# Expert rows added to gathered residual rows in each block, instead of a combine stage at the end

## What is computed

```python
h = rms_norm(x, g_norm_ffn) * (1 + sc_m) + sh_m
g_prob, g_idx = top_k(softmax(h @ w_router_group), 1)       # 1 of 4 groups
e_prob, e_idx = top_k(softmax(logits of this group), 2)     # 2 of its 8 experts
weight = g_prob * e_prob / sum(e_prob)
y[token] += weight * (silu(h @ w_gate[e]) * (h @ w_up[e])) @ w_down[e]   # both experts
x = x + gt_m * y                                            # gate gt_m: one row for prompt, one for sample
```

## Time and profile before

| | us |
|---|---|
| median of 3 runs | 1254.57 (1252.77 to 1256.62) |
| profiled execution | 1249.39, of which the span of the trace is 1247.6 |
| TensorE busy | 1070.9 (86% of the span) |
| VectorE, ScalarE, GpSimd busy | 554.3, 252.5, 186.9 |
| mean granted clock of TensorE | 0.924 |

### The profile page before, as it was taken

One profiled execution on the slowest core, in us unless ns is written; L12 is line 12 of the kernel. 1 busy time (PEld: TensorE's weight loads), 2 busy tenths in 40 slices (PEclk: granted clock), 3 DMA queues, 4 the chain that ended last, 5 costly groups with the idle time before them and its releaser, 6 DMA issues. The chain is left out here.

```text
span 1247.6 us, 13856 instructions
## 1 busy us (share of the span) xinstructions
PE 1070.9 (86%) x4732; PEld 690.1 (55%) x4732; DVE 554.3 (44%) x1110; ACT 252.5 (20%) x595; POOL 186.9 (15%) x267
## 2 busy tenths in 40 slices
PE   4699999999298889989999994399999999999920
PEld 1245555544255455657666753377777777777610
DVE  2345556554363555566575736511222121222147
ACT  1132232222222222332223201011111111111100
POOL 1122222222501101110110000110110011011032
PEclk9799999999677999999999985599999999999975
DMA  8985555441331122221120105649999999999857
GB/s 316 335 304 195 190 189 188 171 154 44 116 88 59 33 78 76 77 93 35 59 74 4 51 34 222 250 155 363 361 375 368 359 371 374 360 363 369 303 193 262
DMA packets 66860, 249.94 MB, mean 200 GB/s; under 512 B 11555, under 2 KB 15286, under 8 KB 51062
## 3 DMA queue, kind: packets, MB, share of 16 engines
q1 hardware_dynamic: 56208, 219.72, 47.5%
q0 software_dynamic: 7216, 26.22, 6.0%
q10 hardware_dynamic: 3382, 3.32, 0.8%
HBM read 195.58 MB, written 53.65 MB: 200 GB/s over the span
## 5 line engine op out<-in xcount | busy, mean ns | idle before, releaser
L903 PE MATMUL bank<-W_in,hT 128*128 128x512 f32 (+3 forms) x432 | 181.3, 573 | 3.4 <-ACTq L1295 3.4
L1061 PE MATMUL bank<-W_out,mT 128*128 128x512 f32 (+1 forms) x288 | 139.7, 618 | 2.9 <-DVEq L1487 2.9
L903 PEld LDWEIGHTS bank<-W_in,hT 128*128 128x128 f32 (+1 forms) x432 | 79.7, 187 | 94.6 <-issue 89.0
L1178 PE MATMUL bank<-WG,xT 128*128 128x256 f32 x528 | 121.3, 383 | 2.4 <-ACT xT L1435 1.9
L1196 PE MATMUL bank<-WD,hidT 128*128 128x512 f32 x264 | 119.0, 593 | 1.6 <-DVE hidT L1961 1.6
L1180 PE MATMUL bank<-WU,xT 128*128 128x256 f32 x528 | 119.3, 379 | 0.0
L1953 DVE TENSOR_TENSOR hid<-sg,bank 128x256 f32<-128x256 f32 x33 | 20.0, 605 | 214.6 <-ACT sg L1442 114.3
L759 POOL TENSOR_SCALAR st<-st 128x1 f32<-128x1 f32 (+6 forms) x77 | 17.7, 230 | 611.9 <-DVEq L1493 611.9
L1180 PEld LDWEIGHTS bank<-WU,xT 128*128 128x128 f32 x528 | 100.3, 190 | 13.6
L1178 PEld LDWEIGHTS bank<-WG,xT 128*128 128x128 f32 x528 | 98.9, 192 | 15.6 <-ACT xT L1435 2.5
L1037 PEld LDWEIGHTS bank<-vall,probT 128*128 128x128 f32 (+1 forms) x656 | 79.2, 190 | 22.0 <-issue 17.9
(11 more groups left out here) (255 smaller groups left out, 1265.8 us busy)
## 6 DMA issues: line engine op xcount, KB each, us to landing
WG<-in_w_gate_e SPq DMA_DIRECT2D x33, 1024.0 KB, 6.0
WU<-in_w_up_e SPq DMA_DIRECT2D x33, 1024.0 KB, 8.0
WD<-in_w_down_e SPq DMA_DIRECT2D x33, 1024.0 KB, 9.7
ada_w<-in_w_ada SPq DMA_DIRECT2D x24, 1024.0 KB, 7.8
expert_rows_scratch<-yb SPq DMA_DIRECT2D x33, 512.0 KB, 3.7
expert_rows_scratch<-zeros SPq DMA_DIRECT2D x8, 1024.0 KB, 11.4
kbuf<-k_scratch SPq DMA_DIRECT2D x12, 384.0 KB, 5.2
xbuf<-in_x_prompt SPq DMA_DIRECT2D x8, 512.0 KB, 3.8
```

What stands on the lines that cost most here:

```text
L903: ins = mm(ps[:R, 0:n], hT[:, t % 2, k, :R], W_in[:, k, c0:c0 + n], start=(k == 0), stop=(k == KD - 1))
L1061: ins = mm(psum[6][:R, :], mT[:, k, :R], W_out[:, k, half * 512:(half + 1) * 512], start=(k == 0), stop=(k == KD - 1))
L1178: mm(psum[2][:, 0:DE], xT[:, k, :], WG[:, slot, k, :], start=(k == 0), stop=(k == KD - 1))
```

## The change

There is no `expert_rows_scratch` and no combine stage. In the attention stage the residual rows x2 are stored twice, to two scratches. Blocks are taken in another order, expert 0 of each of the 4 groups, then expert 1 of each, and so on; since a token's two experts are in one group, both of its slots are in blocks of the same parity, at least 4 blocks apart. Blocks of even number use the first scratch, of odd number the second. For each block GpSimd gathers the residual rows of its tokens to `acc`, VectorE multiplies the down-projection by a gate tile that already holds the row weights (`gate_w`, two buffers) and adds it to `acc`, and GpSimd scatters the sum: the rows whose token has its other slot still to come go back to the scratch, the others to the outputs, prompt rows by one DMA and sample rows by another. Rows that do not belong to a list have an index out of range. The gate tile of a block is made by ScalarE (prompt gate row times weight) and completed by VectorE (sample gate row times weight, added). The row lists for this are made in the routing stage. Rows without a token are no longer gathered; they have an index out of range. The first overflow block is block 33 of the same loop; because it can hold tokens of both parities, its rows are gathered from both scratches. Further overflow blocks, of which these inputs have none, follow as before.

The core of the diff:

```diff
 def overflow_blocks(eng, n_ov, block):
-    with eng.If(n_ov > 0):
-        block(0)
-    with eng.Else():
-        eng.nop()
     with eng.If(n_ov > 1):
...
+NS = NE + 1
...
-    yb_d = nc.dram_tensor("expert_rows_scratch", (YROWS, D), F32).ap()
+    z_d = [nc.dram_tensor(f"residual_scratch{i}", (TOK, D), F32).ap() for i in range(2)]
...
+    TOKEN, EVEN, ODD, FIRST, PROMPT_ROW, SAMPLE_ROW = range(6)
+    ids = sb("ids", [P, 6, NB], I32)
+    roww = sb("roww", [P, 2, NB])
...
+    gate_w = sb("gate_w", [P, 2, D])
+    acc = sb("acc", [P, 2, D])
...
# store_tail (SP)
-        sp.dma_start(x2_d[P * t:P * t + R], x_att[:R, s % 2]).then_inc(s_st2[f"x2_{s % 2}"], 16)
+        for z in z_d:
+            sp.dma_start(z[P * t:P * t + R], x_att[:R, s % 2]).then_inc(s_st2[f"x2_{s % 2}"], 16)
...
# stage 1 (SP)
-                sp.dma_start(yb_d[z:z + ZROWS].rearrange("(p j) (a n) -> p (j a) n", p=P, a=2),
-                             zeros[:].unsqueeze(1).broadcast_to([P, 2 * ZROWS // P, D // 2])).then_inc(s_zst, 16)
...
# expert stage (SP)
+        for b in range(SLOTS):
+            load_expert(b % NG * EG + b // NG, b)
         sp.wait_ge(s_tab, 1)
         with sp.Fori(0, (NE - SLOTS) // SLOTS) as i:
             for u in range(SLOTS):
-                store_y(i * SLOTS + u, u % 2)
                 sp.wait_ge(s_down, i * SLOTS + u + 1)
-                load_expert_dyn(i * SLOTS + (SLOTS + u), u)
+                load_expert_dyn(i + (u * EG + 1), u)
...
# expert stage (GpSimd)
+        do(g.memset(xg[:], 0.0))
+        do(g.memset(acc[:], 0.0))
         g.wait_ge(s_tab, 1)
...
+        def tokens(par, idx):
+            g.indirect_dma_start(xg[:, par], None, h2_d, U(idx), bounds_check=TOK - 1, oob_is_err=False).then_inc(s_xg[par], 16)
+        def rows_in(par, z, idx):
+            g.indirect_dma_start(acc[:, par], None, z, U(idx), bounds_check=TOK - 1, oob_is_err=False).then_inc(s_acc[par], 16)
+        def first_rows_out(par, z, idx):
+            g.indirect_dma_start(z, U(idx), acc[:, par], None, bounds_check=TOK - 1, oob_is_err=False).then_inc(s_zsc[par], 16)
+        def last_rows_out(par, prompt_idx, sample_idx):
+            g.indirect_dma_start(y_p[0], U(prompt_idx), acc[:, par], None, bounds_check=SEQ - 1, oob_is_err=False).then_inc(s_ysc, 16)
+            g.indirect_dma_start(y_s[0], U(sample_idx), acc[:, par], None, bounds_check=DEC - 1, oob_is_err=False).then_inc(s_ysc, 16)
...
+        for b in range(NS):
+            if b + 4 < NS:
+                g.wait_ge(s_xTp, b + 3)
+                tokens(b % 2, at(TOKEN, b + 4))
+            if b:
+                g.wait_ge(s_zsc[(b - 1) % 2], 16 * ((b - 1) // 2 + 1))
+                g.wait_ge(s_ysc, 32 * b)
+            if b + 1 < NE:
+                rows_in((b + 1) % 2, z_d[(b + 1) % 2], at(TOKEN, b + 1))
+            if b + 1 == NE:
+                rows_in(0, z_d[0], at(EVEN, NE))
+            g.wait_ge(s_sum, b + 1)
+            if b == NE:
+                for z in z_d:
+                    first_rows_out(0, z, at(FIRST, b))
+            else:
+                first_rows_out(b % 2, z_d[b % 2], at(FIRST, b))
+            last_rows_out(b % 2, at(PROMPT_ROW, b), at(SAMPLE_ROW, b))
+            if b + 1 == NE:
+                g.wait_ge(s_zsc[1], 16 * (NE // 2))
+                g.wait_ge(s_acc[0], 16 * (NE // 2 + 1))
+                rows_in(0, z_d[1], at(ODD, NE))
...
# TensorE, down and the last regular blocks
-                pe.wait_ge(s_ya, b)
-                pe.wait_ge(s_yv, b)
+                pe.wait_ge(s_yv, b * 2)
...
-        for b in range(NE - SLOTS, NE):
+        for b in range(NE - SLOTS, NS):
...
# ScalarE
-        def y_half(b, par, nth):
-            act.wait_ge(s_down, b + 1)
...
-            A(yb[:, par, 0:512], psum[5][:], ACT.Copy, scale=ww).then_inc(s_ya, 1)
+        def gate(b, par, free):
+            if free is not None:
+                act.wait_ge(s_yv, free)
+            ww = roww[:, 0, b:b + 1] if isinstance(b, int) else roww[:, 0, bass.ds(b, 1)]
+            A(gate_w[:, par], gate_m[:, 0], ACT.Copy, scale=ww).then_inc(s_gw, 1)
...
+        with act.Fori(0, (NE - 2) // 2) as i:
+            for u in range(2):
+                b = i * 2 + u
+                silu(b + 1)
+                gate(b + 2, u, i * 4 + (2 * u + 2))
+                xT_half(b + 2)
+        for b in range(NE - 2, NS - 1):
             silu(b + 1)
-            xT_half(b + 2)
-            y_half(b, b % 2, None)
+            if b + 2 < NS:
+                gate(b + 2, b % 2, 2 * (b + 1))
+            if b + 2 < NS:
                 xT_half(b + 2)
...
# VectorE, routing
+            do(TT(tokf[:, kk, :], posf[:, kk, :], posf[:, 1 - kk, :], ALU.is_lt))
+            do(V.scalar_tensor_tensor(tokf[:, kk, :], tokf[:, kk, :], FIRST_BIT, tok_id[:], ALU.mult, ALU.add))
...
+        do(V.tensor_copy(ids[:, TOKEN, :], idf[:]))
+        signal(s_tab)
...
# VectorE, experts
-            V.tensor_scalar(yb[:, par, 512:], psum[6][:], ww, None, ALU.mult).then_inc(s_yv, 1)
+        def gate(b, par):
+            dve.wait_ge(s_gw, b + 1)
...
+            V.scalar_tensor_tensor(gate_w[:, par], gate_m[:, 1], ww, gate_w[:, par], ALU.mult, ALU.add).then_inc(s_gated, 1)
...
+        def add_rows(b, par, k, nth):
...
+            dve.wait_ge(s_down, b + 1)
+            for half in range(2):
+                c = slice(half * 512, (half + 1) * 512)
+                V.tensor_tensor(yb[:, c], psum[5 + half][:], gate_w[:, par, c], ALU.mult).then_inc(s_yv, 1)
+            dve.wait_ge(s_yv, b * 2 + 2)
+            dve.wait_ge(s_acc[k], nth)
+            V.tensor_tensor(acc[:, k], acc[:, k], yb[:], ALU.add).then_inc(s_sum, 1)
...
+        def steady(b, u, nth):
             hidT_(b)
+            gate(b, u % 2)
             hidden(b + 1)
             xT_half(b + 2)
-            y_half(b, b % 2, None)
+            add_rows(b, u % 2, u % 2, nth)
...
-            do(V.tensor_tensor(y1b[:R, p], y1b[:R, p], y2b[:R, p], ALU.add))
-            do(V.tensor_tensor(y1b[:R, p], y1b[:R, p], gate_m[:R, v], ALU.mult))
-            do(V.tensor_tensor(x2_all[:R, t], y1b[:R, p], x2_all[:R, t], ALU.add))
-            signal(s_yo)
```

More of the change, by code:

```diff
@@ L46 @@
 NB = NE + MAXOV
-YROWS = NB * P
-ZROWS = MAXOV * P // NT
-assert ZROWS * NT == MAXOV * P and ZROWS % P == 0
+NS = NE + 1
+FAR = 65536.0
+FIRST_BIT = 2048.0
 ADA_PARTS = 4
@@ L308, in build_in @@
     bf = sb("bf", [P, 2, NT + 1])
+    far = sb("far", [P, NB])
+    number = sb("number", [P, NB])
+    first = sb("first", [P, NB])
+    idf = sb("idf", [P, NB])
+    odd = sb("odd", [P, MAXOV])
+    odd_i = sb("odd_i", [P, MAXOV], I32)
+    tokf = sb("tokf", [P, 2, NT + 1])
+    assert cursor[0] <= nc.sbuf_usable_end, cursor[0]
     s_params = sem("params_loaded")
@@ L521, in build_in @@
     s_down = sem("down_done")
[L522 to L529, removed]
+    s_gw = sem("prompt_gate_weighted")
+    s_gated = sem("row_gates_ready")
+    s_yv = sem("down_read")
+    s_acc = [sem(f"residual_rows_gathered{i}") for i in range(2)]
+    s_sum = sem("rows_summed")
+    s_zsc = [sem(f"residual_rows_scattered{i}") for i in range(2)]
+    s_ysc = sem("output_rows_scattered")
+    s_over = sem("overflow_step_passed")
     ctx_block = nc.Block()
@@ L683, in load_expert_dyn @@
             sp.dma_start(WD[:, slot], w["w_down_e"][0, bass.ds(e, 1)].rearrange("o (p k) n -> (o p) k n", k=2)).then_inc(s_wd[slot], 16)
-        def store_y(b, par):
-            sp.wait_ge(s_ya, b + 1)
-            sp.wait_ge(s_yv, b + 1)
-            sp.dma_start(yb_d[bass.ds(b * P, P)] if not isinstance(b, int) else yb_d[b * P:(b + 1) * P], yb[:, par]).then_inc(s_yst[par], 16)
-        for e in range(SLOTS):
-            load_expert(e, e)
+        for b in range(SLOTS):
+            load_expert(b % NG * EG + b // NG, b)
         sp.wait_ge(s_tab, 1)
@@ L825, in _ @@
-        gather(0, 0, True)
-        gather(1, 1, True)
-        with g.Fori(0, (NE - 2) // 2) as i:
-            do.off = i * 2
-            for u in range(2):
-                gather(i * 2 + (2 + u), u, False)
-        do.off = 0
-        pool_step.n += (NE - 2) // 2 * 2 - 2
+        g.wait_ge(s_rs, n_roots)
+        g.sem_inc(s_end2, 1)
+        g.wait_ge(s_end2, 5)
+        do(g.memset(xg[:], 0.0))
+        do(g.memset(acc[:], 0.0))
+        g.wait_ge(s_tab, 1)
+        U = lambda idx: bass.IndirectOffsetOnAxis(idx.bitcast(U32), 0)
@@ new lines, in _ @@
+        at = lambda kind, b: ids[:, kind, b:b + 1]
+        tokens(0, at(TOKEN, 0))
+        tokens(1, at(TOKEN, 1))
+        rows_in(0, z_d[0], at(TOKEN, 0))
+        for b in (2, 3):
+            g.wait_ge(s_xTp, b - 1)
+            tokens(b % 2, at(TOKEN, b))
+        g.wait_ge(s_tab, 2)
+        for b in range(NS):
[20 more added lines that the diff above has]
+                rows_in(0, z_d[1], at(ODD, NE))
```

203 lines of the change are left out of this document (86 added, 117 removed).

## The result

The changed kernel takes 1357.43 us (median of 4 runs, 1351.61 to 1357.78) against 1253.67 of the kernel before (4 runs, 1247.03 to 1256.62): the ratio is 1.0825, with a 95% interval of 1.0772 to 1.0877. The forecast was 1377, in a range from 1317 to 1417. The profiled execution took 1357.45 us with a span of 1355.6, which is 108.1 more than the profiled execution before.

The account below looks back on a forecast made before the run. TensorE, never free in the expert stretch, was taken to bound the kernel. 1249.4 - 34.5 (end) + 103.2 (ScalarE's order) + 52.7 (clock) + 1.1 (routing) = 1371.9, plus 5.2 from profiled execution to median: 1377, range 1317 to 1417.

Parts of the forecast that it names:

- case A: Expert loop: TensorE waits on a chain through ScalarE's queue and its clock falls; 1377 us in total, chance 0.70.
- part 1: End of the kernel, from the second last regular down-projection: 77.2 us become 42.7, a gain of 34.5 (28 to 38).
- part 4: Routing ahead of the expert loop: added VectorE operations and strided writes, less an index copy; +1.1 us (-0.5 to +3).
- Part 2: Expert loop: ScalarE's xT copy queues behind the gate's wait for VectorE's products; TensorE waits 3.44 us per block, +103.2 (96 to 111).
- Part 3: Expert loop: TensorE's clock falls after each idle gap, 1.7 us per block over 31 blocks, +52.7 (0 to 93).
- Rival B: Expert loop: the chain stalls TensorE but its clock stays full, 1324 us; 1417 if 3.0 us lost per block; chance 0.19.
- costed at nothing: Second residual store, GpSimd's memsets, dropped zero stores, VectorE's work, GpSimd's 10 us loop and DMA under the block: no cost.
- rival C: Expert loop: GpSimd's loop binds as well through slow scatters, some 2 us more per block, about 1439 us; chance 0.06.
- Rival D: Expert loop: the gate's wait ends before TensorE wants xT, so no stall per block; faster, 1218 us; chance 0.05.

Follow-up runs that it names:

- the two orders: ScalarE's xT copy moved behind its half of y in the kernel before, 1297.9 us; xT copy moved ahead of the gate in the changed kernel, 1265.57 us.
- the four gate tiles: Changed kernel with four gate_w tiles instead of two, ScalarE's order kept, so the gate waits for products of two blocks earlier: 1261.26 us.
- the kernel with the copy ahead: Changed kernel with ScalarE's order silu, xT copy, gate, instead of silu, gate, xT copy: 1265.57 us, 1.0136 of the kernel before.
- four sums: Changed kernel with xT copy before gate, four acc tiles instead of two, one scatter semaphore per tile, rows gathered for block b+2: 1220.12 us, 0.9741 of the kernel before.

## Why the prediction was right

It said 1377 and named case A, the chain and the fallen clock; 1357 is this case. It was 20 us too high. The clock's term was 20.8 too large, the chain's 3.9, and 5.2 were added for a distance between the median and the profiled execution that was nil here; part 1 was 2.3 too hopeful and part 4 took 7.6 too little. So the term of the clock alone has the size of the miss, and the other errors cancel.

- Part 1, the end: -33.1 against -34.5. The forecast had counted the overflow block's transposes, 0.9, in this part, though they now stand ahead of it; like for like it is -32.2. The direction and what goes away were right, the closeness is partly luck. The landings were shorter than taken: a scatter lets go 3.3 us after its issue once the weights are loaded (issued at 1321.88, GpSimd released at 1325.15), and the last gather's rows are there 3.4 us after its issue (1336.97, VectorE's addition at 1340.36), against 5.0 each. The last scatter's landing ends GpSimd's wait 2.5 us after its issue began at 1346.33, at 1348.87 (forecast 5.7). In return the sum had nothing behind that landing, where 6.7 us follow until the end at 1355.6; 5.15 of them are a drain of GpSimd, from 1350.20, an instruction recorded in the trace and not among the busy ones. Before, GpSimd's drain began at 1229.59 and was over at 1240.0, beside the combine stage's last operations. The last down-projection's wait of 2.85 us for VectorE's hidT cost nothing: its products were done 3.3 us before the last rows came.
- Part 2, the order on ScalarE: 3.31 us per block against 3.44, so 99.3 against 103.2. The mechanism is shown by the two orders and the four gate tiles. The products started 3.73 us after the down-projection (forecast 3.79) and took 1.29 together, not 1.40; the gate took 1.15, as forecast. The chain came to 6.83 against 7.09, and the first products after a gap take 0.1 longer, which the forecast had not.
- Part 3, the clock: 31.9 against 52.7. This is the mis-sized term. The price of a fall was right (1.68 against 1.7). That it falls in every block was not: from one gap of 2.90 us with a fall and one of 1.68 without, I took a gap of 3.1 to be past the point where it always happens. At this length it happens in 19 of 31 blocks; of the lengths tried only 4.2 us had it in all of them. The rule of "TensorE: Matmul & The Clock Gate" in the Trainium skill, section "Why this matters for your kernels", which warns against such gaps, holds in kind, but as a share of the gaps and not in each: 12 falls at 2.6 us, 19 at 3.1. Rival B (no fall) is excluded by the 19 falls, its upper case (3.0 us in each block) by their price.
- Part 4, what stands ahead of the loop: +8.7 against +1.1. The terms given there add up to 0.8 and not to 1.1 (0.8 for four operations, 0.4, 0.7, less 1.1), which changes nothing here. Routing has 3.2 of the 8.7, outside its bound of +3 by little; 1.6 are the memset on VectorE's first operation, which I had costed at nothing because GpSimd was free: with the memsets held back routing is 1.5 and 1.7 us longer than before, about as forecast. The other 5.4 lie in the attention stage: the first weight load after it is issued at 769.7 instead of 764.2. The clock was at 0.50 twice there, once more than in the earlier trace rows (table by stage, kernel after):

```profile
722.60:726.00 3.40, 3.40 (x18) 3.40 (x18) 0.00 (x0) 0.00 (x0) 0.00 (x0) 0.50 0.00 0
736.30:743.10 6.80, 6.22 (x8) 2.60 (x9) 3.68 (x3) 0.21 (x2) 0.79 (x2) 0.50 0.51 204
```

The nine other kernels here with the doubled store reached the same weight load 3.3 us earlier to 2.7 us later than the kernel before, seven of them earlier. So the 5.4 are not shown to be the change's, and no cost of the doubled store is to be seen. Over all twelve kernels this time goes with how long the clock was at 0.50 in the attention stage after 700 us: 761.0 and 761.5 where it never was, 762.3 to 763.7 with 3.4 us of it, 763.5 to 766.9 with 6.8, and 769.7 with the 13.6 us of the kernel after. That order fits a clock that takes its share of the 5.4; what makes it fall there in one kernel and not in the next isn't shown.

- What was costed at nothing: the cover of GpSimd's loop held in the kernel after, though with a smaller margin than I wrote. I took 5.0 us for the landing of a scatter from a gather of token rows in the trace before. It is 8.1 us in the median and 10.4 at most here (answer for the tile acc, kernel after: gathers and scatters of residual rows together, where the trace has their landing), and the first scatter's issue 1.86 instead of 0.94:

```profile
L789 POOL DMA_INDIRECT residual_scratch<-acc,ids x34: 985/1857/1878, 844.0 to 1343.8; - x34
...
DMA to landing us min/median/max: 2.1/8.1/10.4
```

In the five turns of the kernel with the copy ahead, above, the loop is 12.0 to 15.2 us: mostly under a block of 14.7, and over one of 11.44. I had named the condition (slow landings) and the wrong place for it: rival C is no addition to case A but what appears once part 2 is repaired. Rival D's price of 1218 needed both repairs: the order alone gives 1265.6, order and four sums 1220.1.

## What to carry to other kernels

Before an operation with a new wait is put into an engine's queue, look at what is queued behind it and who needs that: here one line's place in ScalarE's queue cost 3.3 us in each block, and more by the clock, while ScalarE's new work itself cost nothing. After such a repair, measure the next loop again at the new, shorter period; what a block of 14.7 us covers, one of 11.44 may not. And take a landing time from transfers that meet the same load: beside some 300 GB/s of mostly weights the next gather came 8.6 us after the last scatter's issue in the median, and without most of them 3.6 at most.

## What the runs showed of the hardware that I had not expected

- The fall of the clock after a recurring gap is a matter of share: at 0.5 and 1.3 us of idle time per block in none of the 31 blocks, at 2.6 in 12, at 3.1 in 19, at 4.2 in all 31, at 1.7, 1.7 and 2.0 us each. Once, at 722.6 us in the kernel after, it fell though TensorE was busy without a gap from 712.0 to 722.6.
- A memset of GpSimd, 1.80 us, held up an operation of VectorE on 8 columns for as long, in eight kernels of eight.
- GpSimd's drain at the end of the program took 5.15 us in the kernel after, 5.95 with four sums, and 10.44 in the kernel before, where it lay beside other work. What sets its length isn't shown.
- The software queue's packets rose from 7216 to 24048 with about the same bytes (26.22 and 26.81 MB): rows that are left out through an index out of range are not free of packets. By size, 6528 of the 24048 packets carry 4096 bytes and 17520 carry 4, against 6400 and 816 before. Before, the 4-byte ones are 16 for each of 51 indirect DMAs; at 16 for each of the 167 after, 14848 are left, and that is the number of row places left out: 167 x 128 - 6528. What one of them costs wasn't measured by itself.

```profile
q0 software_dynamic: 7216, 26.22, 6.0%
```
